# Moving the last third of each unit's merge steps ahead of the value product in the differential attention loop

## The reference, cut to what matters

```python
def block(qb):
    s = jnp.einsum('qbhid,bkhid->bhiqk', qb, k).astype(jnp.float32) * scale
    p = jax.nn.softmax(s, axis=-1)
    a = (p[:, :, 0] - lam * p[:, :, 1]).astype(v.dtype)
    return jnp.einsum('bhqk,bkhd->qbhd', a, v)
...
g = jax.nn.sigmoid(u_gate).reshape(B, L, N_BRANCH, D_MODEL)
merged = (g[:, :, 0] * (y_hy @ w_lift[0]) + g[:, :, 1] * (y_na @ w_lift[1])
          + g[:, :, 2] * (y_da @ w_lift[2]))
```

## Time and profile before

| what | value |
|---|---|
| median of 3 runs | 2854.18 us |
| lowest and highest run | 2850.81 and 2856.85 us |
| the profiled execution | 2850.32 us, span 2848.5 us |
| PE busy | 2664.7 us, 94% of the span |
| DVE, POOL, ACT busy | 1980.3, 1447.3 and 943.1 us |
| stage of the 40 units | from 637 to 893 us in layer 0, from 1956 to 2213 us in layer 1 |

### The profile page before, as it was taken

One profiled execution on the slowest core, in us unless ns is written; L12 is line 12 of the kernel. 1 busy time (PEld: TensorE's weight loads), 2 busy tenths in 40 slices (PEclk: granted clock), 3 DMA queues, 4 the chain that ended last, 5 costly groups with the idle time before them and its releaser, 6 DMA issues.

```text
span 2848.5 us, 42903 instructions
## 1 busy us (share of the span) xinstructions
PE 2664.7 (94%) x16712; PEld 2426.5 (85%) x16712; DVE 1980.3 (70%) x3018; ACT 943.1 (33%) x1873; POOL 1447.3 (51%) x620
## 2 busy tenths in 40 slices
PE   7959899999998999999998989998999998999998
PEld 2329687989988998999997869797988898999998
DVE  6676687676676558888777578567676566765866
ACT  3542112334553125242242112314554114332432
POOL 0436132274444774666665505065444675566654
PEclk9979999999999999999998999999999999999999
DMA  5423243131112423324222216033111331222222
GB/s 224 155 92 96 85 156 119 67 119 45 55 54 96 161 74 102 121 82 126 89 82 81 92 59 233 12 113 95 55 55 54 132 122 54 81 90 75 82 84 80
DMA packets 81590, 274.23 MB, mean 96 GB/s; under 512 B 9035, under 2 KB 15819, under 8 KB 79468
## 3 DMA queue, kind: packets, MB, share of 16 engines
q1 hardware_dynamic: 48124, 168.77, 19.2%
q10 hardware_dynamic: 33264, 102.72, 10.3%
HBM read 247.86 MB, written 23.59 MB: 95 GB/s over the span
## 4 chain that ended last, share of the span: by engine, by line
PE 64%; DVE 17%; DVEq 5%; issue 4%; ACT 4%; DMA 3%; POOLq 1%; POOL 1%; ACTq 0%; SPq 0%
PE PS L607 33%; PE PS L1084 8%; PE PS L945 6%; PE PS L993 3%; DMA wraw<-in_w_strips 2%; PE PS L668 2%; DVEq L2182 2%; PE PS L893 2%; DVE bsum L2183 2%; PE PS L617 1%; DVE adap L1709 1%; PE PS L813 1%; PE PS L877 1%; PE PS L829 1%; DVE dp L2045 1%
## 5 line engine op out<-in xcount | busy, mean ns | idle before, releaser
L575 POOL TENSOR_SCALAR whi<-wraw 128x1024 fp32r<-128x1024 f32 x188 | 551.7, 2935 | 923.1 <-PE PS L607 480.0
L577 POOL TENSOR_TENSOR wlo<-wraw,whi 128x1024 fp32r<-128x1024 f32 x212 | 557.3, 2629 | 89.1 <-ACT whi L1373 59.9
L1709 DVE CUSTOM_DVE_ANT_0 adap<-ada,cond 128x1024 f32<-128x1024 f32 x176 | 316.0, 1795 | 33.1 <-DMA ada<-in_w_ada 12.2
L607 PE MATMUL PS<-hhi,whi 128*128 128x320 f32 x1152 | 265.8, 312 | 11.9 <-POOL wlo L577 11.6
L607 PE MATMUL PS<-hlo,whi 128*128 128x320 f32 x1152 | 264.1, 310 | 0.0
L607 PE MATMUL PS<-hhi,wlo 128*128 128x320 f32 x1152 | 263.8, 310 | 0.0
L588 POOL TENSOR_TENSOR blo<-bsum,bhi 128x512 fp32r<-128x512 f32 x120 | 176.7, 1479 | 171.0 <-ACT bhi L1574 171.0
L2141 DVE SCALAR_TENSOR_TENSOR x<-PS,mod,x 128x128 f32<-128x128 f32 (+2 forms) x240 | 90.9, 434 | 176.4 <-PE PS L607 174.5
L607 PEld LDWEIGHTS PS<-hhi,whi 128*128 128x128 f32 x1152 | 193.7, 189 | 14.6 <-POOL wlo L577 12.9
L1084 PE MATMUL PS<-hhi,bhi 128*128 128x320 f32 x640 | 199.3, 311 | 3.5 <-DVE blo L2189 1.5
L1084 PE MATMUL PS<-hhi,blo 128*128 128x320 f32 x640 | 197.8, 309 | 0.0
(11 more groups left out here) (340 smaller groups left out, 7000.6 us busy)
## 6 DMA issues: line engine op xcount, KB each, us to landing
wraw<-in_w_strips SPq DMA_DIRECT2D x292, 512.0 KB, 3.6
ada<-in_w_ada ACTq DMA_DIRECT2D x80, 512.0 KB, 4.6
spectra<-hst ACTq DMA_DIRECT2D x48, 256.0 KB, 2.6
cond<-conds ACTq DMA_DIRECT2D x7, 1024.0 KB, 6.3
hld<-spectra ACTq DMA_DIRECT2D x8, 768.0 KB, 5.1
hld<-spectra ACTq DMA_DIRECT2D x12, 512.0 KB, 3.6
part<-hacc ACTq DMA_DIRECT2D x8, 640.0 KB, 4.3
macc<-part ACTq DMA_DIRECT2D x8, 640.0 KB, 4.1
```

The lines of the kernel that those rows point to most:

```text
L575: nc.gpsimd.tensor_scalar(hi, raw, 1.0, None, ALU.mult)
L577: nc.gpsimd.tensor_tensor(lo, raw, hi, ALU.subtract).then_inc(w_split, 1)
L607: ins = pe.matmul(out[:, h, :], w[:, kt, :], mv[:, h * HALF:(h + 1) * HALF], start=start and m == 0, stop=stop and m == 2)
L1709: ins = V.tensor_tensor_reduce(adap[s][:, :], ada[s][j][:, :], cond[s][:, c, :], 1.0, 0.0, ALU.mult, ALU.add, mraw[:, 2 * m + c:2 * m + c ...
```

## The change

In each iteration PE issued a third of the merge steps after the scores, a third after the turn and the rest after the value product. Now it issues the first third after the scores and all the rest between the turn and the value product. Nothing stands between the value product of one iteration and the scores of the next. The queues of the other engines are not edited.

```diff
                     if n:
                         da_turn(n - 1)
-                    for j in range(j0 + more // 3, j0 + 2 * more // 3):
+                    for j in range(j0 + more // 3, j0 + more):
                         merge_step(j)
                     if n:
                         da_pv(n - 1)
-                    for j in range(j0 + 2 * more // 3, j0 + more):
-                        merge_step(j)
                 for j in range(steps_before(40), 384):
                     merge_step(j)
```

## The result

The changed kernel takes 2881.45 us, median of 7 runs (2869.77 to 2886.78), beside 2853.82 us for the kernel before on the same chip (7 runs, 2850.23 to 2858.38). The ratio is 1.0096, with a 95% interval of 1.008 to 1.0112: slower by 27.6 us. The forecast was 2881. The profiled execution took 2882.25 us.

What follows compares the result with a forecast made beforehand. PE's instruction order was taken to bound the 256 us unit stage of each layer; -12.4 + 9.6 + 12 + 4.1 = +13.3 us per layer, +26.6 for two, on 2854.2 gave 2881 us, range 2854 to 2902.

Steps and rivals of the forecast that it cites:

- plain wait: PE's turn waiting for DVE's difference, without lateness: 1.11 us in 7 short iterations, 1.78 in iteration 40; 9.6 us per layer.
- stretched instructions: DVE differences and factors lengthened by POOL's split at L577, and late outputs, now paid at PE's turn: +12 us per layer.
- The gain: Value product on PE no longer waits for ACT's copy of the turned map: -12.4 us per layer, between 8.9 and 17.4.
- The turn: PE's turn, wanted sooner after the value product, waits for DVE's difference: 9.6 us plain plus 12 us for lateness per layer.
- the cushion forecast: Time to spare at PE's turn in a full iteration: cut from 1.85 us to 0.12 us.
- The banks: Moved merge steps wait for ACT's gate activation in iterations 3, 14, 37, slightly more in 32: 4.1 us per layer.
- The clock: Rival, 10%: waits at PE's turn lower the granted clock, about 2 us per place; 2893 us, or 2909 at the upper bound.
- the bank wait of 1.62 us: Existing wait of merge steps for the gate's activation in iteration 32, forecast to grow by some 0.3 us.
- POOL falls into the gaps: Rival, 10%: splits at L577 meet DVE while it waits for PE, so stretching leaves the differences; faster, 2844 us.
- No change: Rival, 10%: lateness at PE's turns stays as it was, third term about 0; +1.3 us per layer, 2857 us.

## Why the prediction was right, point by point

PE's timeline gives the distance of each instruction from the one ahead. Summed by kind over the stage, and compared with the kernel before, it makes this table in us per layer. The forecast at the turn is 9.6 for the plain wait and 12 for the stretched instructions:

| term | forecast | layer 0 | layer 1 |
| --- | --- | --- | --- |
| value product's wait for the copy | -12.4 | -12.4 | -12.7 |
| waits at the turn | +21.6 | +18.7 | +19.3 |
| merge steps that wait for the gate | +4.1 | +4.1 | +4.0 |
| merge steps at the low clock | 0 | +4.7 | +2.0 |
| the rest | 0 | +0.5 | -1.7 |
| sum | +13.3 | +15.6 | +10.9 |

The rest is what a block of another kind takes: products that have not waited are shorter, scores behind them longer, and steps start again less often.

**The gain** was the middle of two totals that measure the same wait in different ways, 8.9 and 17.4, and it met the start-to-start distances of 18.3 before and 5.9 after. The weight loads' total was too high and the matmuls' too low.

**The turn.** The plain wait was forecast at 1.11 us in a short iteration and is 1.24 (1.91 less 0.67), and 1.9 for 1.78 in iteration 40: together 10.6 for 9.6. My distance from product to next scores was 1.25 us and is 1.03, since I had left in it what goes with the wait and the steps: a product that has waited takes 1.10 us, one that has not 1.00, and the first step behind a product starts 0.09 us late. The next scores take 0.09 us longer for it (0.83 for 0.74). A full iteration keeps about the cushion forecast, 0.12 us: the difference ends 1.84 us behind the scores, the turn starts at 1.99.

**The stretched instructions** were forecast at +12, with bounds 0 and 20. What is left of the turn's row is 18.7 - 10.6 = 8.1 and 8.7. The pair of kernels without the subtraction gives 18.3 - 7.5 = 10.8 per layer in the stages, but with the clock in it. The mechanism was right and its size some 3.6 too large. It was also put down to L577 alone, but in the kernel before some 4 us of the stretching lie beside L575. I had charged nearly every stretched instruction in full; some fell in iterations where nothing at the turn was due.

**The banks** came out by iteration and by size; only in iteration 32 did the wait grow by 0.5 us for the 0.3 forecast.

**The clock** was a rival with 10% and stood at nothing in the sum. It fell behind waits at the turn (and one for the gate), in five places of layer 0 and two of layer 1, at 0.6 to 1.5 us each, and cost 3.4 us per layer in merge steps. The fall in iteration 40 is not in this: in layer 1 it cost about 2 us more, at the last value product (2.15 us to the first step behind it, for 1.14) and at some ten matmuls behind it, 0.12 us each. Without POOL's subtraction the low clock costs the changed kernel 2.4 and 1.5 us per layer, no more than the kernel before (2.2 and 1.8): it follows the stretched differences. The price per place was under the 2 us of the rival. This is the step of the prediction that was wrong: the bank wait of 1.62 us, from which I took that waits in the middle of the stage leave the clock alone, was not long enough to stand for these. That its 3.4 us and the 3.6 of the term before cancel is luck; so is it that the layers, +15.6 and +10.9, have their mean at the forecast 13.3, and that the medians of the runs, 27.6 us apart, lie nearer to the forecast 26.6 than the profiled executions with 32.0. The total was forecast nearer than its parts.

**The rivals.** *POOL falls into the gaps*: refuted, the sum of stretching moved only from 16.5 to 15.0 us. *No change*: refuted by the ratio. What remains open is why the clock held behind other waits of the same length: in iteration 17 the turn comes 4.03 us behind the scores in layer 0 and 4.02 in layer 1, and the product then 5.22 and 3.69 us behind the turn. No run here varies a wait at a fixed place.

## What to carry to other kernels

When work is moved out of a gap on one engine, ask what the work in that gap covered on another: the four steps behind the value product had hidden DVE's output and difference, and without them what was late on DVE or POOL became PE's time. Look in each in-order queue for an instruction that needs nothing of the wait it stands behind; here its exchange with the one ahead turned the same move from 27.6 us lost into one worth 20 us, and the two edits have to be tried together, since alone the one loses and the other gives only a third. Here the wait's total by weight loads (17.4 us) was too high and that by matmuls (8.9) too low; the distances from start to start gave it (12.4).

## What the runs showed of the hardware

A POOL MEMSET of 128x1024 (0.95 us) never held up DVE's two-input instructions, 32 of which ran in part beside one, where the subtraction in its place had made single factors up to 2.33 us long in the changed kernel. Beside L575, which reads SBUF as well, most such instructions kept their time, too: a difference at 772.88 us took 0.89 us while L575 ran from 771.74 to 774.51, in the changed kernel without the subtraction. But a few were longer all the same. Timeline of the kernel before, on DVE and POOL:

```profile
692.46 0.95 DVE L2040 SCALAR_TENSOR_TENSOR coef<-sums,rsum,lamt 128x1 f32<-128x1 f32 x1
693.48 0.89 DVE L2045 SCALAR_TENSOR_TENSOR dp<-dp,coef,dp 128x640 f32<-128x640 f32 x1
...
692.36 2.77 POOL L575 TENSOR_SCALAR whi<-wraw 128x1024 fp32r<-128x1024 f32 x1 [6.03 <-PE PS L945]
```

The factor ends 1.05 us behind the start of L575, and the difference behind it runs undisturbed although L575 goes on to 695.13. This repeats in the traces of all ten executions: beside an L575 of 2.77 us, only factors and differences that started from 0.02 us ahead of it to 0.62 us into it were over 0.1 us too long, and each of these factors ended 1.05 us behind its start, each difference 1.72 us (three factors beside an L575 of 3.46 us ended 1.74 us behind its start). So L575 held DVE up in its first part only. A stretched factor beside L577 ended with it, a stretched difference about 0.7 us behind its end (753.69 for 753.01 in the iteration shown). Why L575 lets go early is open; no run here varies it.

A value product whose weights had been ready took 1.00 us for its eight matmuls, one that had waited 1.10; scores directly behind a product took 0.83, behind merge steps 0.74. Such differences of 0.1 us, 40 times in a layer, are as large as some of the waits that were forecast.
